# Two-block transformer on one core: high and low words of stationary weight tiles woven word by word

## The reference

```python
def pool_layer(x, mem, norm_g, w_in, w_pool, pool_scale, mem_g, w_mem_kv, w_out):
    h = rmsnorm(x, norm_g)
    proj = h @ w_in
    ...
    return x + jnp.concatenate([y_pool, y_mem], axis=-1) @ w_out

def second_block(x, attn_norm, w_qkv, ...):
    ...
    h = rmsnorm_2(x, ffn_norm[l])
    g = causal_dwconv(jnp.einsum('bsd,df->bsf', h, w_gate[l]), conv_w[l], conv_b[l])
    u = jnp.einsum('bsd,df->bsf', h, w_up[l])
    x = x + jnp.einsum('bsf,fd->bsd', jax.nn.silu(g) * u, w_down[l])
    return rmsnorm_2(x, final_norm)
```

## Time and profile before

| | us |
|---|---|
| median of two runs | 2037.74 |
| the two runs | 2035.72 and 2039.75 |
| span of the profiled execution | 2037.8 |
| TensorE busy in it | 2019.6 |
| VectorE busy | 1452.9 |
| ScalarE busy | 1036.3 |
| GpSimd busy | 415.8 |

### The profile page before, as it was taken

How to read it: one execution, slowest core, us unless ns; L and a number is a source line. 1 busy time by engine, 2 the same in 40 slices (tenths; PEclk the granted TensorE clock), 3 DMA queues, 4 the chain that set the end, 5 groups by cost and what they waited for, 6 DMA issues and landing times.

```text
span 2037.8 us, 29295 instructions
## 1 busy us (share of the span) xinstructions
PE 2019.6 (99%) x11506; PEld 1763.8 (87%) x11506; DVE 1452.9 (71%) x2056; ACT 1036.3 (51%) x1548; POOL 415.8 (20%) x376
## 2 busy tenths in 40 slices
PE   8999999999999999999999999999999999999998
PEld 7888888888888888888878888888888888888887
DVE  6866788788796556876656678777776567777755
ACT  6744544566433554644555555455454344545443
POOL 0014553300000344430122235211010000101122
PEclk9999999999999999999999999999999999999999
DMA  9664556567654334555444445555556655555664
GB/s 339 218 193 151 193 186 196 184 226 239 210 182 145 114 114 135 187 203 189 152 161 141 154 149 190 183 191 190 190 190 187 190 191 190 192 191 192 183 189 145
DMA packets 104809, 374.22 MB, mean 184 GB/s; under 512 B 11840, under 2 KB 13152, under 8 KB 104288
## 3 DMA queue, kind: packets, MB, share of 16 engines
q1 hardware_dynamic: 104384, 371.83, 54.8%
q10 hardware_dynamic: 288, 0.52, 0.1%
HBM read 370.21 MB, written 2.10 MB: 183 GB/s over the span
## 4 chain that ended last, share of the span: by engine, by line
PE 94%; DVE 3%; DMA 1%; ACT 1%; POOL 0%; issue 0%; DVEq 0%; SPq 0%; ACTq 0%
PE psg L554 50%; PE psg L555 26%; PE psg L621 2%; PE psg L623 2%; PE psg L622 2%; PE psg L595 1%; PE pst L595 1%; DVE s_w L1726 1%; PE pst L752 1%; PE psg L598 1%; PE pst L598 1%; PE pss L843 1%; PE pst L660 1%; DMA s_stage<-in_mk 1%; PE pso L863 1%; ACT s_w L1156 0%
## 5 line engine op out<-in xcount | busy, mean ns | idle before, releaser
L1726 DVE TENSOR_TENSOR s_w<-s_stage,s_w 128x1024 fp32r<-128x1024 f32 (+3 forms) x698 | 861.4, 1236 | 350.8 <-ACT s_w L1156 348.0
L1156 ACT ACTIVATE s_w<-s_stage 128x1024 fp32r<-128x1024 f32 (+3 forms) x698 | 727.0, 1043 | 730.6 <-PE psg L555 633.6
L554 PE MATMUL psg<-s_ry,s_w 128*128 128x512 f32 x2560 | 900.4, 394 | 1.8 <-DVE s_qc L1780 1.8
L555 PE MATMUL psg<-s_ry,s_w 128*128 128x256 f32 x2560 | 723.2, 283 | 0.0
L554 PEld LDWEIGHTS psg<-s_ry,s_w 128*128 128x128 f32 x2560 | 482.5, 188 | 108.0 <-issue 2.3
L555 PEld LDWEIGHTS psg<-s_ry,s_w 128*128 128x128 f32 x2560 | 485.8, 190 | 0.4
L554 PE MATMUL psg<-s_rh,s_w 128*128 128x512 f32 x1216 | 428.0, 394 | 0.3 <-DVE s_w L1726 0.3
L555 PE MATMUL psg<-s_rh,s_w 128*128 128x256 f32 x1216 | 342.7, 282 | 0.0
L554 PEld LDWEIGHTS psg<-s_rh,s_w 128*128 128x128 f32 x1216 | 228.3, 188 | 49.0 <-issue 1.0
L554 PE MATMUL psg<-s_hid,s_w 128*128 128x512 f32 x704 | 244.1, 390 | 0.0
L555 PEld LDWEIGHTS psg<-s_rh,s_w 128*128 128x128 f32 x1216 | 229.8, 189 | 0.7
(11 more groups left out here) (417 smaller groups left out, 2203.4 us busy)
## 6 DMA issues: line engine op xcount, KB each, us to landing
s_stage<-in_wo SPq DMA_DIRECT2D x96, 512.0 KB, 3.6
s_stage<-in_wg SPq DMA_DIRECT2D x84, 512.0 KB, 3.5
s_stage<-in_wu SPq DMA_DIRECT2D x84, 512.0 KB, 3.9
s_stage<-in_ain SPq DMA_DIRECT2D x64, 512.0 KB, 3.7
s_stage<-in_wd SPq DMA_DIRECT2D x64, 448.0 KB, 3.3
s_stage<-in_wkv SPq DMA_DIRECT2D x32, 512.0 KB, 3.6
s_stage<-in_wd SPq DMA_DIRECT2D x32, 512.0 KB, 3.4
s_stage<-in_bq SPq DMA_DIRECT2D x24, 512.0 KB, 3.6
```

What stands on the lines that cost most here:

```text
L554: e.matmul(o, M.WH[:, r, ws], xx, start=begin, stop=False)
L555: m = e.matmul(o[:, T:2 * T], M.WL[:, r, ws], xh, start=False, stop=end)
L1156: e.activation(M.weights(c, 0, n, shift), M.staged(c, n), ACT.Copy).then_inc(S["wh"], 1)
L1726: e.tensor_tensor(M.weights(c, 1, n, shift), M.staged(c, n), M.weights(c, 0, n, shift), ALU.subtract).then_inc(S["wl"], 1)
```

## The change

Only the places of the words in the three slots change, and only for units with stationary tiles of 128 words (616 of the 699). Their high and low words now stand side by side: word 2i of a tile is the high word i, word 2i + 1 the low word i. A tile takes 256 words and 4 more that stay empty, TW = 260 words = 1040 bytes, so tile n begins 16n bytes further modulo 256. A slot is SLOT = 2144 words = 8576 bytes = 33.5 x 256, so slots 0 and 2 begin at 128 and slot 1 at 0 modulo 256. A weight load takes every second word: step 8 bytes instead of 4. ScalarE writes, and VectorE reads and writes, with the same step; the staged words that they read stay packed. The low words of tile n begin 4 bytes after the high ones.

`shift=None` marks a woven unit; pair, cw1, cw2 and gate units keep their flat form within the new slots, so in slot 1 they lie 128 bytes away modulo 256 from where they were. The slots' tensor is 256 bytes smaller, so all tensors behind it move by 256 bytes and keep their remainders.

The instructions of all five engines stand in the same order as before, with the same waits. The only differences of the two listings are the shapes of the copies and subtractions (128x8x128 in place of 128x1024), beside the line numbers: L554 and L555 are L571 and L572 after the change.

```diff
--- before.py
+++ after.py
@@ -20,6 +20,8 @@
 NS = 4
 NR = 3
 UWP = UW + 64
+TW = 2 * 128 + 4
+SLOT = 2144
 SHIFT = 8
 NTOT = 699
 WINS = (2, 4, 8, 16)
@@ -185,7 +187,7 @@
         self.counts = {"out": 0, "out_act": 0}
         self.between = iter(())

-    def unit(self, ap, n, shift=0):
+    def unit(self, ap, n, shift=None):
         self.units.append((ap, n, shift))

     def take(self, tile):
@@ -249,7 +251,7 @@
             for _ in range(3 if w == 0 else 0):
                 yield
             for m in range(8):
-                self.unit(self.A["cw1"][8 * w + m], 1024)
+                self.unit(self.A["cw1"][8 * w + m], 1024, 0)
                 self.zb.append(len(self.units))
                 if m == 7:
                     self.close(("cw1", w), None)
@@ -258,7 +260,7 @@
                     yield
             for _ in range(6):
                 yield
-            self.unit(self.A["cw2"][w], 256)
+            self.unit(self.A["cw2"][w], 256, 0)
             self.close(("cw2", w), None)
             yield

@@ -356,10 +358,7 @@

         self.ST = fix("stage", [128, NS, UW])

-        slots = fix("w", [128, NR, 2 * UWP], F32R)
-        self.W = slots[:, :, :].rearrange("p r (s c) -> p r s c", s=2)
-        self.GW = slots[:, :, 0:KT * 72].rearrange("p r (k c) -> p r k c", k=KT)
-        self.WH, self.WL = self.W[:, :, 0, :], self.W[:, :, 1, :]
+        self.SLOTS = fix("w", [128, NR * SLOT + 32], F32R)
         self.X = fix("x", [128, KT, T])
         self.C = fix("cons", [128, NCON])
         self.V = fix("vec", [128, NVEC])
@@ -484,17 +483,36 @@

     def gate_weights(self, r):

-        return self.GW[:, r, :, :]
+        return self.SLOTS[:, r * SLOT:r * SLOT + KT * 72].rearrange("p (k c) -> p k c", k=KT)
+
+    def flat(self, r):
+
+        return self.SLOTS[:, r * SLOT:r * SLOT + 2 * UWP].rearrange("p (s c) -> p s c", s=2)
+
+    def woven(self, r, part, a, b):
+
+        t = self.SLOTS[:, r * SLOT + a * TW:r * SLOT + b * TW].rearrange("p (t w) -> p t w", w=TW)
+        return t[:, :, part:256:2]
+
+    def high(self, r, n):
+        return self.woven(r, 0, n, n + 1)[:, 0, :]
+
+    def low(self, r, n):
+        return self.woven(r, 1, n, n + 1)[:, 0, :]

     def weights(self, c, part, n, shift):

         if n == KT * 36:
             return self.gate_weights(c % NR)[:, :, 36 * part:36 * part + 36]
-        return self.W[:, c % NR, part, shift:shift + n]
-
-    def staged(self, c, n):
+        if shift is None:
+            return self.woven(c % NR, part, 0, n // 128)
+        return self.flat(c % NR)[:, part, shift:shift + n]
+
+    def staged(self, c, n, shift):
         s = self.ST[:, c % NS, 0:n]
-        return s.rearrange("p (k c) -> p k c", k=KT) if n == KT * 36 else s
+        if n == KT * 36:
+            return s.rearrange("p (k c) -> p k c", k=KT)
+        return s.rearrange("p (t w) -> p t w", w=128) if shift is None else s

     def hid(self, part):

@@ -547,12 +565,11 @@
         if c:
             w.wait_ge("wl", c + 1)
         for kk in range(nk):
-            ws = slice(kk * mw, kk * mw + mw)
             ready(k0 + kk)
             xh, xx, _ = x(k0 + kk)
             begin, end = first and kk == 0, last and kk == nk - 1
-            e.matmul(o, M.WH[:, r, ws], xx, start=begin, stop=False)
-            m = e.matmul(o[:, T:2 * T], M.WL[:, r, ws], xh, start=False, stop=end)
+            e.matmul(o, M.high(r, kk), xx, start=begin, stop=False)
+            m = e.matmul(o[:, T:2 * T], M.low(r, kk), xh, start=False, stop=end)
         m.then_inc(S["units"], 1)

     def tile(t, x, ready, sizes=(8, 8), k0=0, mw=128):
@@ -582,7 +599,6 @@
             else:
                 steps = [(kk, p, 4 * kk + p) for p in (2, 3, 0, 1) for kk in range(2)]
             for k, p, n in steps:
-                ws = slice(128 * n, 128 * n + 128)
                 if k == 0:
                     vacant(P.bank[tiles[p]])
                     held[P.bank[tiles[p]]] = P.out[tiles[p]]
@@ -592,10 +608,10 @@
                 xh, xx, _ = x(k)
                 if c == 0:
                     w.wait_ge("wh" if n >= 4 else "wh_a", 1)
-                e.matmul(o[:, :], M.WH[:, r, ws], xx, start=k == 0, stop=False)
+                e.matmul(o[:, :], M.high(r, n), xx, start=k == 0, stop=False)
                 if c == 0:
                     w.wait_ge("wl" if n >= 4 else "wl_a", 1)
-                m = e.matmul(o[:, T:2 * T], M.WL[:, r, ws], xh, start=False, stop=k == 15)
+                m = e.matmul(o[:, T:2 * T], M.low(r, n), xh, start=False, stop=k == 15)
             m.then_inc(S["units"], 1)
             if hook is not None and u == 3:
                 hook()
@@ -618,9 +634,10 @@
                 xh, _, xl = x(k)
                 ts, ws = slice(128 * i, 128 * i + 128), slice(SHIFT + 512 * kk, SHIFT + 512 * kk + 512)
                 o = M.product(banks[i])
-                e.matmul(o[:, :], xh[:, ts], M.WH[:, r, ws], start=(k == 0), stop=False)
-                e.matmul(o[:, :], xh[:, ts], M.WL[:, r, ws], start=False, stop=False)
-                m = e.matmul(o[:, :], xl[:, ts], M.WH[:, r, ws], start=False, stop=(k == 15))
+                wh, wl = M.flat(r)[:, 0, ws], M.flat(r)[:, 1, ws]
+                e.matmul(o[:, :], xh[:, ts], wh, start=(k == 0), stop=False)
+                e.matmul(o[:, :], xh[:, ts], wl, start=False, stop=False)
+                m = e.matmul(o[:, :], xl[:, ts], wh, start=False, stop=(k == 15))
                 if u == 7 and n == 1:
                     m.then_inc(S["half"], 1)
             m.then_inc(S["units"], 1)
@@ -722,8 +739,8 @@
                 o = M.PST[:, 0, 0:T] if i == 2 else M.PSO[i][:, 0:T]
                 vacant(bank)
                 for k in range(3):
-                    ws = slice(((i - a) * 3 + k) * 128, ((i - a) * 3 + k + 1) * 128)
-                    m = three(o, M.WH[:, r, ws], M.WL[:, r, ws], (M.RP[g % 2][:, 0, k, :], M.RP[g % 2][:, 1, k, :]), k == 0, k == 2)
+                    n = (i - a) * 3 + k
+                    m = three(o, M.high(r, n), M.low(r, n), (M.RP[g % 2][:, 0, k, :], M.RP[g % 2][:, 1, k, :]), k == 0, k == 2)
                 if i == 0:
                     m.then_inc(S["wp0"], 1)
                 held[bank] = ("y_w", YAT["pool"] + 3 * g + i + 1)
@@ -749,7 +766,7 @@
                 zb = M.ZB[m % 3]
                 for i in range(4):
                     ws = slice(i * 256, i * 256 + 256)
-                    x = e.matmul(M.PST[:, 0, :], zb[:, i, :], M.W[:, r, :, ws], start=(m == 0 and i == 0), stop=(m == 7 and i == 3))
+                    x = e.matmul(M.PST[:, 0, :], zb[:, i, :], M.flat(r)[:, :, ws], start=(m == 0 and i == 0), stop=(m == 7 and i == 3))
                 x.then_inc(S["units"], 1)
                 done[0] += 1
                 yield
@@ -773,13 +790,14 @@
             for k in range(2):
                 ws = slice(k * 128, k * 128 + 128)
                 hh, hl = M.HT[:, 0, k, :], M.HT[:, 1, k, :]
+                wh, wl = M.flat(r)[:, 0, ws], M.flat(r)[:, 1, ws]
                 o = M.PSO[0][:, 0:128]
                 if v == 0:
-                    x = three(o, M.WH[:, r, ws], M.WL[:, r, ws], (hh, hl), k == 0, k == 1)
+                    x = three(o, wh, wl, (hh, hl), k == 0, k == 1)
                 else:
-                    e.matmul(o, hh, M.WH[:, r, ws], start=(k == 0), stop=False)
-                    e.matmul(o, hh, M.WL[:, r, ws], start=False, stop=False)
-                    x = e.matmul(o, hl, M.WH[:, r, ws], start=False, stop=(k == 1))
+                    e.matmul(o, hh, wh, start=(k == 0), stop=False)
+                    e.matmul(o, hh, wl, start=False, stop=False)
+                    x = e.matmul(o, hl, wh, start=False, stop=(k == 1))
             x.then_inc(S["units"], 1)
             done[0] += 1
             held["o", 0] = ("cmp", v + 1)
@@ -1153,7 +1171,7 @@
         w.wait_ge(f"st{c % NS}", 16 * (c // NS + 1))
         if c >= NR:
             w.wait_ge("units", c - NR + 1)
-        e.activation(M.weights(c, 0, n, shift), M.staged(c, n), ACT.Copy).then_inc(S["wh"], 1)
+        e.activation(M.weights(c, 0, n, shift), M.staged(c, n, shift), ACT.Copy).then_inc(S["wh"], 1)

     def nxt(n=1):
         for _ in range(n):
@@ -1210,7 +1228,8 @@

         done[0], ws = 1, slice(512 * half, 512 * half + 512)
         w.wait_ge(("st_a", "st0")[half], 16)
-        e.activation(M.WH[:, 0, ws], M.ST[:, 0, ws], ACT.Copy).then_inc(S[("wh_a", "wh")[half]], 1)
+        src = M.ST[:, 0, ws].rearrange("p (t w) -> p t w", w=128)
+        e.activation(M.woven(0, 0, 4 * half, 4 * half + 4), src, ACT.Copy).then_inc(S[("wh_a", "wh")[half]], 1)

     def mem0(j):
         w.wait_ge(mem_piece(j), 16)
@@ -1723,7 +1742,7 @@
         done[0] += 1
         _, n, shift = P.units[c]
         w.wait_ge("wh", c + 1)
-        e.tensor_tensor(M.weights(c, 1, n, shift), M.staged(c, n), M.weights(c, 0, n, shift), ALU.subtract).then_inc(S["wl"], 1)
```

(8 more changed lines are left out.)

## The result

The changed kernel takes 2063.65 us (2062.33 to 2064.98) against 2037.74 us: a ratio of 1.0122, 95% interval 1.0098 to 1.0147. It is slower, by 26 us, and by less than 2%. The forecast was 2023 us.

A forecast was written before the change was run, and what follows sets the result against it. TensorE's matmul steps were taken to bound the kernel; 2037.8 - 14 (weight loads) + 0 (copy and subtraction) + 0 (flat units) = 2023 us, 0.7% less, called the same, with a range of 2004 to 2110 us.

The forecast's parts named there:

- What bounds the kernel: TensorE, mostly L554 and L555: the step between matmuls times their number, 4800 pairs x 0.347 = 1664 us.
- (a): Weight loads of woven tiles at step 8 bytes: 3 ns less a pair, 14 us less; half the possible gain.
- The bound of +12 from L798: Upper bound on weight loads by place: both products 6 ns longer, as at L798's median; 58 us more.
- The rate bound: Upper bound on weight loads at half rate: 214 ns a load, 256-column step at least 225, 514 us more.
- (b): ScalarE's copy and VectorE's subtraction at step 8 bytes keep the packed rate; cost 0, hidden anyway.
- rival of slow steps: Strided VectorE and ScalarE access slows: 2140 us at 1.83 ns a column, about 2500 at 2.6; chance 13%.
- (c): Flat units keep their form, a third move 128 bytes modulo 256: taken as 0, at worst 3 us.
- bad places: Rival: some start offsets make equal-speed streams collide; 3 to 12 ns a pair, 2052 to 2095 us; 12%.
- no effect: Rival: interference is set by something other than the step; 2038 us; chance 12%.
- half-rate loads: Rival: woven weight loads run at half the rate; 2038 + 514 = 2550 us; chance 4%.
- much faster: Rival: the ten extra ns were interference after all, a pair gains 19 ns; 91 us less, 1947 us; 7%.
- The test I had set for the step: Forecast falls if a pair steps by less than 0.338 or more than 0.356 us.

The follow-up runs named there:

- experiment 1: Changed kernel with every woven tile in every slot at 128 modulo 256 bytes, as before the change: 2068.82 us, ratio 1.0148.
- experiment 6: Kernel before, with only the high words of two neighbouring tiles woven with each other (step 8 bytes), low words packed: 2059.53 us, ratio 1.0096.
- experiment 9: Memory of experiment 5, but low tiles go against 512 columns and high tiles against 256: 2055.12 us, ratio 1.0081.
- experiment 5: Kernel before, with only the low words of two neighbouring tiles woven with each other (step 8 bytes), high words packed: 2039.98 us, ratio 1.0004.
- experiment 2: Packed words as in the kernel before, but tiles and slots at the changed kernel's remainders modulo 256: 2050.07 us, ratio 1.0058.
- experiment 4: Packed words as in the kernel before, all 128-word tiles at 160 modulo 256, the activations' remainder: 2049.68 us, ratio 1.0054.
- experiment 7: As experiment 5, but low words of four tiles woven together, so low-tile loads step 16 bytes: 2175.45 us, ratio 1.0664.
- experiment 8: Packed words as in the kernel before, all 128-word tiles at 224 modulo 256: 2067.49 us, ratio 1.0135.
- experiment 12: Packed words as in the kernel before, high tiles at 128 modulo 256, low tiles moved to 160: 2050.34 us, ratio 1.0056.
- experiment 10: Kernel before, packed at 128, with both products of the pair at 512 columns, adding the term wl x xl: 2571.31 us.

## Why the prediction was wrong

**What bounds the kernel** was right. The whole difference is 4800 pairs times a difference of step (from one start to the next), and the way of counting gives 26 of 26 us.

**(a), the weight loads, failed, in its sign.** I took 3 ns a pair less; measured were 5.4 more, so the term that I had at -14 us was +26. The bound of +12 from L798 held. Two steps of the working were wrong. The first was the mechanism: that two operands which advance equally fast stay apart and so stop costing. In experiments 1, 6 and 9 equal speed is the worse case (235.8 ns against 228.5), and with a load of the same step beside the 512-column product (experiment 5) it makes no difference at all. The second was the picture of how much is left to gain. I read 388 ns, the middle of L621's durations, and 278, from one product beside which no load runs, as the level that a good layout approaches, and took the kernel before as an ordinary case between good and bad. L621 to L623 promise less than their 387 to 389 say: their median step is 227 ns, but their average, 228.8, is no better than L554's 228.5. The table shows the kernel before as the best of eleven on average, and 256-column products with a load beside them reached 274 (experiment 6), under the supposed floor, while their 512-column neighbours lost more. The two products of a pair have to be counted together.

The row with the right sign was in the prediction: L798, where places changed from tile to tile, at a median of 396. That is what the changed kernel's 512-column products have. That the number is the same is luck: L798's loads are packed, and packed tiles on changing places gave 393 (experiment 2); the rest came with the step of 8 bytes. I made it an end of the range, and took L621 as the nearest row because its operands had equal remainders; experiment 4 gave the stationary tiles that remainder and lost 11 us.

**The load's duration** was forecast at 188 and is 194 to 197. The rate bound (214 ns at half the rate) was far off for step 8; experiment 7 shows that about this loss of rate comes with step 16. No run had it beside the 256-column product, for which the 514 us were worked out.

**(b), the copy and the subtraction.** Cost 0, as taken. VectorE's part was right also in detail (1251 against 1247). ScalarE's duration was not: 7% more, hidden as the prediction said, behind TensorE releasing slots. VectorE shows the packed rate at step 8 and 1.82 ns a column at step 16, where each 16-byte line is hit once. Of the two rules of the Trainium skill, the one of "SBUF — State Buffer", section "Specifications (TRN2)", two accesses in each 16-byte line, agrees with that. The one of the Trainium skill's "Vector Engine (DVE) Microarchitecture Reference", section 5.2, asks for two adjacent words, which step 8 does not give, and step 8 ran at the packed rate all the same; the 1.82 of step 16 does lie in the range that it gives for single words. Moving packed tiles changes the 512-column step by 6 ns (228.5 at 128, 234.9 at 224). The Trainium skill's "SBUF — State Buffer", section "Who interferes with whom", TensorE never waiting for another reader, cannot explain that.

At 1.82 ns a column experiment 7 also comes close to the rival of slow steps, which I had worked out for 1.83: 2140 us. Measured were 2175, of which 56 are the longer steps of the pair, which that rival did not have.

**(c), the flat units**, at 0: the three products of `pair` went from 228.8 to 230.2 ns on average, 768 x 1.4 = 1 us.

**The rivals.** Of those written down, "bad places" comes nearest, with the right size (3 to 12 ns a pair) and a chance of 12%, far too little. Its cause is half right: places alone cost 12 us (experiment 2), but with places as before the woven kernel is slower still (experiment 1). The argument for "no effect", one step for all tiles and slots, tells nothing: where all tiles have one remainder, the slower kernels of experiments 1 and 8 have one step as well, 236 and 235. The rivals of slow steps on VectorE, half-rate loads and "much faster" did not come. The test I had set for the step, below 0.338 or above 0.356 us, was so wide that 0.3526 passed it; the durations, with 396 in place of "below 390" and loads of 194 in place of 188, did refute the forecast.

**What stays open.** Why a stepped load beside the 256-column product stretches the next product by 7 ns and leaves the same load beside a 512-column one free; why the pair on packed tiles at 128 loses its 228 ns when both its products have 512 columns; what puts a stretch of experiment 12 into one way of running or another. The runs show when, not by what. Since the same layout can run at 344.4 or 353.3 ns a pair, the places alone do not set the step, and the average of such a layout depends on how long each way lasted. A test would start the same products after waits of different lengths.

## What to carry to other kernels

In this kernel, where products follow each other without a gap, the layout of the stationary operand alone was worth up to 1.5%, and no other layout tried was faster than the one that it was built around: where a layout was tuned, expect a change to lose by it unless a row shows the new one. Price such a change by the rows where the same property varies (here the 72-column tiles), not by the lowest durations, and count both products of a pair. Look at the steps stretch by stretch before an average is taken for the property of a layout. Step 8 bytes for 4-byte words was free for VectorE, cost ScalarE's copy 7% and a load 3 to 5%; step 16 cost far more.

## What the runs showed of the hardware

- A weight load of 128 float32r columns lasts 188 ns with step 4 bytes, 194 to 198 with step 8, 309 with step 16 (medians; experiments 5, 6, 7).
- VectorE's subtraction of 1024 columns: 1247 ns packed, 1251 when one operand and the output have step 8, 2017 when the output has step 16. ScalarE's copy: 1059 packed, 1135 with an output of step 8.
- Moving all packed stationary tiles by 96 bytes, with the same instructions, costs 28 us of 2039 (experiment 8).
- The 512-column product of 228.5 ns becomes one of 234.0 when the product after it has 512 columns instead of 256 (experiment 10), in the same memory layout; products of 512 columns in turn with the activations stationary keep their median duration of 389 (L621).
- The cost of a stepped load falls on the product behind the one that it starts beside, where that one has 256 columns (experiments 6 and 9: 228.5 to 235.8 ns, while the 256-column product gets 3 ns shorter).
- The same line, operands and layout stepped by 344.4, 346.7 and 353.3 ns a pair in different stretches between waits of one execution (experiment 12).
